# Turning softmax probabilities with a diagonal of reciprocal sums instead of the identity, in a two-block attention kernel

## The reference

```
s = einsum('bqhgd,bkhd->bhgqk', qg, k) * d ** -0.5      # + window mask, bias or sink column
p = softmax(s, axis=-1)
o = einsum('bhgqk,bkhd->bqhgd', p, v)
```

## Time and profile before

| | |
|---|---|
| median of 3 runs | 1799.63 us (1799.13 to 1804.88) |
| the profiled execution | 1798.95 us |
| its span | 1797.2 us |
| PE busy | 1690.1 us (94%) |
| DVE busy | 1037.0 us (58%) |
| ACT busy | 834.2 us (46%) |

### The profile page before, as it was taken

One profiled execution on the slowest core, in us unless ns is written; L12 is line 12 of the kernel. 1 busy time (PEld: TensorE's weight loads), 2 busy tenths in 40 slices (PEclk: granted clock), 3 DMA queues, 4 the chain that ended last, 5 costly groups with the idle time before them and its releaser, 6 DMA issues.

```text
span 1797.2 us, 30868 instructions
## 1 busy us (share of the span) xinstructions
PE 1690.1 (94%) x12106; PEld 1488.1 (83%) x12106; DVE 1037.0 (58%) x1965; ACT 834.2 (46%) x1546; POOL 81.7 (5%) x90
## 2 busy tenths in 40 slices
PE   4999989999999989997799999988999998989998
PEld 1985566888888869974699999868999998789998
DVE  3436644634343454358565656665867657568775
ACT  3327744513232333236444445674545546755443
POOL 2100001000000012110000001000000000000000
PEclk8999999999999999999999999999999999999999
DMA  8818763433333333347356663613666536046662
GB/s 246 218 48 260 233 176 97 114 95 103 95 94 95 105 108 104 110 135 226 83 147 179 180 187 106 182 36 102 182 187 188 148 112 195 12 141 179 182 190 85
DMA packets 406255, 254.48 MB, mean 142 GB/s; under 512 B 8448, under 2 KB 405024, under 8 KB 406112
## 3 DMA queue, kind: packets, MB, share of 16 engines
q1 hardware_dynamic: 404576, 248.80, 47.3%
q0 software_dynamic: 1536, 3.71, 0.8%
HBM read 251.36 MB, written 1.11 MB: 140 GB/s over the span
## 4 chain that ended last, share of the span: by engine, by line
PE 88%; DVE 6%; ACT 3%; issue 2%; DMA 2%; SPq 0%; DVEq 0%; ACTq 0%
PE bank L2143 72%; PE bank L2353 3%; PE bank L2364 3%; PE bank L2374 2%; PE bank L2266 2%; PE bank L2154 2%; PE bank L2122 2%; DVE parts L1118 1%; PE bank L2348 1%; DMA H<-ctx_t 1%; PE bank L2380 1%; PE bank L2389 1%; ACT parts L1301 1%; PE bank L2299 1%; DMA raw<-ada_w 0%
## 5 line engine op out<-in xcount | busy, mean ns | idle before, releaser
L2143 PE MATMUL bank<-AT,parts 128*128 128x256 f32 (+1 forms) x4704 | 680.1, 307 | 14.7 <-DVE AT L1104 7.6
L2143 PEld LDWEIGHTS bank<-AT,parts 128*128 128x128 f32 x4704 | 636.2, 192 | 56.9 <-issue 18.2
L1301 ACT ACTIVATE parts<-raw 128x1024 fp32r<-128x1024 f32 (+1 forms) x368 | 368.8, 1040 | 333.9 <-PE bank L2143 319.5
L1118 DVE TENSOR_TENSOR parts<-raw,parts 128x1024 fp32r<-128x1024 f32 (+1 forms) x368 | 434.9, 1213 | 147.0 <-ACT parts L1301 146.9
L2143 PE MATMUL bank<-HID,parts 128*128 128x256 f32 (+1 forms) x2592 | 400.2, 316 | 9.1 <-DVE HID L1800 9.1
L2143 PEld LDWEIGHTS bank<-HID,parts 128*128 128x128 f32 x2592 | 367.1, 192 | 40.3 <-DVE HID L1800 9.7
L2143 PE MATMUL bank<-parts,AT 128*128 128x256 f32 x2112 | 261.6, 285 | 12.3 <-DVE WORK L1935 6.7
L2143 PEld LDWEIGHTS bank<-parts,AT 128*128 128x128 f32 x2112 | 257.9, 193 | 14.7 <-DVE WORK L1935 7.2
L2023 DVE SCALAR_TENSOR_TENSOR H<-bank,MOD,H 128x256 f32<-128x256 f32 x120 | 52.5, 479 | 156.1 <-PE bank L2143 156.1
L1301 ACT ACTIVATE TOK<-bank 128x512 f32<-128x512 f32 (+2 forms) x160 | 71.3, 488 | 143.2 <-PE bank L2143 113.0
L2008 DVE TENSOR_TENSOR PR<-PR 128x512 f32<-128x512 f32 x48 | 33.1, 690 | 114.3 <-ACT PR L1545 114.3
(11 more groups left out here) (199 smaller groups left out, 1267.8 us busy)
## 6 DMA issues: line engine op xcount, KB each, us to landing
raw<-mlp_w SPq DMA_DIRECT2D x128, 512.0 KB, 4.2
raw<-ada_w SPq DMA_DIRECT2D x96, 512.0 KB, 4.8
raw<-w_up SPq DMA_DIRECT2D x88, 512.0 KB, 4.8
raw<-w_in SPq DMA_DIRECT2D x32, 512.0 KB, 4.5
raw<-w_down SPq DMA_DIRECT2D x32, 512.0 KB, 4.3
raw<-odd_w_in SPq DMA_DIRECT2D x24, 512.0 KB, 4.1
raw<-w_out SPq DMA_DIRECT2D x16, 512.0 KB, 4.8
raw<-even_w_in SPq DMA_DIRECT2D x12, 512.0 KB, 9.6
```

Source lines behind the costliest of these rows:

```text
L1118: ng.tensor_tensor(chunk_part(c, 1), chunk_raw(c), chunk_part(c, 0).bitcast(F32), ALU.subtract)\
L1301: return nc.scalar.activation(o, i, ACT.Copy)
L2143: ins = MM(out, stay, move, start=opens and kt == 0 and i == 0, stop=kt == kts - 1 and i == 2 and stops)
```

## The change

The reciprocals move ahead of the turn. For each step DVE takes the reciprocals of its two row sums, and scales the identity by each of them into a diagonal matrix in DIAG (four places of 128 x 128). PE then turns a tile by an ordinary float32 product, tile.T times diagonal, so that the turned probabilities come out normalised. The reciprocals' products in PE, ROOTS, OUT and the multiplication at the output fall away: ACT takes the high part straight from the values' bank, and DVE the low part, in a unit `four_low` that now stands at the head of the next odd iteration, ahead of `diag` and the score maxima. Kind D keeps its transposes.

```
+            if size == 2 and i % 2 and i > 4:
+                add("four_low", st=value)
+            if size == 2 and 0 <= i - 2 < n:
+                y = add("diag", four=steps[i - 2])
...
         if size == 2:
-            add("flush", ("flush", jobs[0]["layer"]), layer=jobs[0]["layer"])
+            add("four_low", st=value)
...
@@ ACT
-                elif k == "value" and x.four or k == "flush":
-                    if k == "value":
-                        filled(act, x.u)
-                        copy(ROOTS[:, x.c % 2, :], b[:, N:2 * N]).then_inc(root_turned, 1)
...
-                        copy(four_to(y, 0), OUT[:, y.c % 4, :]).then_inc(head_high, 1)
+                elif k == "value" and x.four:
+                    filled(act, x.u)
+                    copy(four_to(x, 0), b[:, 0:N]).then_inc(head_high, 1)
...
@@ DVE
-                        V.reciprocal(to, den).then_inc(root_ready, 1)
...
-                        V.tensor_tensor(OUT[:, x.c % 4, :], b[:, 0:N], ROOTS[:, x.c % 2, :], ALU.mult).then_inc(drained, 1)
...
+                elif k == "diag":
+                    for j in x.four:
+                        consumed(dve, index[("score", j["j"], 0)].u)
+                    if x.c >= 2:
+
+                        filled(dve, max(index[("turn_p", j["j"])].u for j in diags[x.c - 2].four))
...
+                    step(V.reciprocal(RD[:, i:i + 2], den))
+                    settle()
+                    for n in range(2):
+                        V.tensor_scalar(diag_of(x, n), ident, RD[:, i + n:i + n + 1], None, ALU.mult)\
+                            .then_inc(diag_ready, 1)
+                elif k == "four_low":
+                    y = x.st
+                    dve.wait_ge(head_high, y.c + 1)
+                    V.tensor_tensor(four_to(y, 1), bank[:, y.u % BANKS, 0:N], four_to(y, 0).bitcast(F32), ALU.subtract)\
+                        .then_inc(bank_drained[y.u % BANKS], 1)
...
@@ PE
-                            consumed(pe, s.u)
+                            n = j["diag"].four.index(j)
+                            pe.wait_ge(diag_ready, 2 * j["diag"].c + n + 1)
...
+                            if j["kind"] == "D":
+                                last = nc.tensor.transpose(b[:, o:o + P], p, ident)
+                            else:
+                                last = MM(b[:, o:o + P], p, diag_of(j["diag"], n), start=True, stop=True)
...
-                    pe.wait_ge(root_ready, x.c + 1)
-                    for v in range(TB):
-                        for i in range(2):
-                            r = roots(x)[1][:, 2 * v + i:2 * v + i + 1].broadcast_to([P, HD])
-                            last = MM(bank[HD * i:HD * i + HD, x.u % BANKS, N + v * P:N + v * P + P], r, ident, start=True,
-                                      stop=True, tile_position=(0, HD * i))
```

More of the change, by code:

```diff
@@ L234, in attention @@
                 add("mix", ("mix", j["j"]), job=j)
+            if size == 2 and i % 2 and i > 4:
+                add("four_low", st=value)
+            if size == 2 and 0 <= i - 2 < n:
+                y = add("diag", four=steps[i - 2])
+                for j in y.four:
+                    j["diag"] = y
             for j in steps[i] if i < n else ():
@@ L490, in plan @@
     for pos, x in enumerate(units):
-        if x.kind not in ("ada_row", "ahead", "post", "tail", "apply", "mix", "soft", "flush", "prep", "rstd", "final"):
+        if x.kind not in ("ada_row", "ahead", "post", "tail", "apply", "mix", "soft", "four_low", "diag", "prep", "rstd", "final"):
             x.u = u
@@ L536, in plan @@
             count["conv"] += 1
+        if x.kind == "diag":
+            x.c = count["diag"]
+            count["diag"] += 1
         if x.kind == "mix":
@@ L795, in two_block_kernel @@
         fours = [x for x in units if x.kind == "value" and x.four]
+        diags = [x for x in units if x.kind == "diag"]
         for x in fours:
@@ L987, in four_to, with fours_of @@
             return AT[:, part, ft, lo:lo + N]
-        def fours_done(layer, ft):
-            return max(x.c for x in fours if x.layer_of == layer and x.ft_of == ft) + 1
+        def fours_of(layer, ft):
+            return [x for x in fours if x.layer_of == layer and x.ft_of == ft]
         def turned_o_to(x):
@@ L1016, in resid_wait @@
                 else:
-                    pe.wait_ge(head_low, fours_done(layer, kt))
+                    for y in fours_of(layer, kt):
+                        consumed(pe, y.u)
             elif x.group[0] == "relu2":
@@ L1969, in _ @@
                     V.scalar_tensor_tensor(p1, p2, ratio, p1, ALU.mult, ALU.add).then_inc(comb_ready, 1)
-                elif k == "turn_p" and x.job["kind"] != "D":
-                    y = x.job["of"]
-                    if x.four[-1] is y.four[-1]:
-                        for j in y.four:
-                            consumed(dve, index[("score", j["j"], 0)].u)
-                        i, to = roots(y)
-                        den = DEN[:, i:i + 4]
-                        if y.job["kind"] in ("A", "CA"):
-                            step(V.tensor_tensor(ES[:, i:i + 4], ES[:, i:i + 4], den, ALU.add))
-                            settle()
-                            den = ES[:, i:i + 4]
-                        V.reciprocal(to, den).then_inc(root_ready, 1)
-                elif k == "value" and x.four or k == "flush":
-                    if k == "value":
-                        filled(dve, x.u)
-                        dve.wait_ge(root_turned, x.c + 1)
-                        V.tensor_tensor(OUT[:, x.c % 4, :], b[:, 0:N], ROOTS[:, x.c % 2, :], ALU.mult).then_inc(drained, 1)
-                        last = [x.c - 2] if x.c - 2 >= index[("value", first_four[x.job["layer"]])].c else []
-                    else:
-                        last = [last_four[x.layer].c - 1, last_four[x.layer].c]
-                    for c in last:
-                        y = fours[c]
-                        dve.wait_ge(head_high, c + 1)
-                        V.tensor_tensor(four_to(y, 1), OUT[:, c % 4, :], four_to(y, 0).bitcast(F32), ALU.subtract)\
-                            .then_inc(head_low, 1)
@@ new lines, in _ @@
+                elif k == "diag":
[3 more added lines that the diff above has]
+                        filled(dve, max(index[("turn_p", j["j"])].u for j in diags[x.c - 2].four))
+                    i = index[("score", x.four[0]["j"], 0)].nm % 8
+                    den = DEN[:, i:i + 2]
+                    if x.four[0]["kind"] in ("A", "CA"):
+                        step(V.tensor_tensor(ES[:, i:i + 2], ES[:, i:i + 2], den, ALU.add))
+                        settle()
+                        den = ES[:, i:i + 2]
+                    step(V.reciprocal(RD[:, i:i + 2], den))
+                    settle()
+                    for n in range(2):
[6 more added lines that the diff above has]
+                        .then_inc(bank_drained[y.u % BANKS], 1)
+                elif k == "value" and x.four:
+                    pass
@@ L2373, in _ @@
                         for i in range(2):
[L2374 to L2381 removed]
+                            last = MM(bank[HD * i:HD * i + HD, x.u % BANKS, 0:N], values_of(x.four[i])[t],
+                                      turned_pair(x, i, t), start=t == 0, stop=t == tiles - 1, tile_position=(0, HD * i))
                 elif k == "value":
```

22 lines of the change are left out of this document (7 added, 15 removed).

## The result

The changed kernel takes 1863.03 us (median of 4 runs, 1860.77 to 1865.19) against 1799.38 for the kernel before (4 runs, 1798.87 to 1804.88). The ratio is 1.0338, with a 95% interval of 1.0318 to 1.0358: slower by 63.6 us, where 48.5 were forecast. The profiled execution took 1864.81 us with a span of 1863.0, 65.8 more than the span before.

What follows compares the result with a forecast made beforehand. PE was taken as the limit before, a ring through DVE and ACT after. Layers 2 and 3 add 24 us and layer 0 24.5, so 48.5 on 1798.95 gives 1847.5, said as 1848; range 1825 to 1864.

Steps and rivals of the forecast that it cites:

- The ring: Attention loop once per four: ACT's values copy, DVE's low part, diagonals, PE's turn, ACT's copy, exponentials; sets the pace, not PE.
- The sign of being wrong that the prediction gave for DVE's row: Score maxima, now behind the diagonals, release the exponentials later than the copies do, making the ring longer than forecast.
- PE's own work: PE in three attention stages: 320 turned tiles add 35.2 us, dropped reciprocals' products save 14.4, so 20.8 us more.
- the forecast's own bounds: Whole kernel 1834 to 1860 us: diagonal 3 us, kind B 5, per-tile price 2, unseen slack 6.
- The ring of kind N, 5.5: Layers 2 and 3, kind N: 1.35 + 1.03 + 0.63 + 1.10 + 1.37 = 5.5 us per four, against 4.0 before.
- The start: Start of layer 3's attention: diagonals about 1.3 us late, first turns 1.8 more at half clock; 3 us.
- Layer 0's groups: Layer 0's attention: groups of kind A 17.4 us, of B some 15.7, against 13.65 before; 24.5 us with start and drain.
- Some slack may be found that my ring does not show: Attention stages: hidden slack might take back a fifth of what the ring adds beyond PE, 6 us.
- Only PE's work: Attention stages: low part never late, so only PE's added work counts; 1820 or 1822 us; chance 0.14.
- Faster: Turn on PE: product's second record hides behind weight loads, diagonals ready in time; saves 14.4 to 17.3 us, 1783; chance 0.05.
- The fourfold tile: Turn on PE: a turned tile costs four times the transpose, 112 us more, 1911; chance 0.02.
- The clock stays low: Layers 2 and 3: gaps at each four keep PE at granted clock 0.50, 31 us more, 1879; chance 0.04.

Runs made afterwards that it cites:

- the square: Kernels before and after plus four variants: turn by transposes or products, with output normalised, nothing normalised, or turn waiting for diagonals; ratios 0.9935 to 1.0338.
- the second look: The changed kernel run again unaltered for a second profile; 1861.95 us in one run, span 1860.2.
- kernel 4: The changed kernel without reciprocals, diagonals or their wait, turned by the product with the plain identity, nothing normalised; 1819.57 us, ratio 1.0104.

## Why the prediction was right and wrong

**The direction, the mechanism and PE's work were right.** The ring was named with its order of links, and in kind N the trace has those, but for the stretch between the two turns, where DVE's row and not PE's is the later path. The sign of being wrong that the prediction gave for DVE's row, maxima that release the exponentials later, did not come: ACT's exponentials wait 6.3 us in all for the maxima in the changed kernel, 15.8 in the kernel before. PE's own work was forecast at 20.8 us; the kernel with that alone came out at 0.0104 x 1800 = 18.7. By stretch it was 13.0, 2.3 and 2.4, where the terms of the prediction give 192 x 0.11 - 16 x 0.45 = 13.9 and twice 64 x 0.11 - 8 x 0.45 = 3.4. The parts were each a little large, and their errors cancel in part: the product costs 0.097 per tile by the square (0.11 forecast), the dropped products and their cover 12.5 us (14.4 forecast). Where PE sets the pace, in layer 0's steady groups, a tile does cost 0.110; the average is lower because in layers 2 and 3 part of the work falls into gaps that PE has anyway.

**The term that was too small is what the ring adds beyond PE's work.** The forecast of 48.5 holds 48.5 - 20.8 = 27.7 for it; the square gives 42. That the time still lies inside the range is in part luck: the forecast's own bounds ended at 1860 (the ones named add up to 10 us, so 1858), and only the step from there to 1864, for which no term was given, takes it in. By stretch, after less work alone, it is 15.0, 11.8 and 14.8 (19.7, 13.1 and 10.5 in the second look), where the prediction had 24.5 - 13.9 = 10.6 and twice 12 - 3.4 = 8.6. Three places make the difference, in the prediction's own steps:

- *The ring of kind N, 5.5.* It is 5.75. My turn until the next scores (1.03) took 1.06, but from the scores to the next turn it is 0.75, not 0.63, since that turn waits for its own diagonals at the end of DVE's row; and its end, copy, exponentials and copy add up to 1.16 + 1.39 = 2.55, not 2.47. From the first values to the last (1587.62 to 1627.04) layer 3 takes 39.4 us against 28.16, so 11.3 more, where 8.5 and 1 for kind M were forecast. The start was right in size: 11.84 us from the second pair of scores (1575.78) to the first values (1587.62), against 9.01, so 2.8 more where I gave 3 (11.04, 2.0 more, in the second look). The end was not: PE waits 1.43 and 0.99 ahead of its last turn and values, and in the first profile the values run at half pace (1.97 instead of 1.08).
- *Layer 0's groups.* Six periods from 148.76 to 251.41 take 102.65 us, 17.1 each, while the mean of my 17.4 and 15.7 is 16.5. (The same six take 83.16 before, 13.9 each and not 13.65, so the growth is 3.2 per group against a forecast mean of 2.9.) Kind A's first two periods are 18.1 and 17.7, not 17.4, its third 16.7. Kind B's are 16.5 to 16.9, not 15.7. PE's work alone takes 15.8 there in kernel 4 (15.4 by my terms), and the wait adds 0.7 to 1.1 where I gave it a few tenths: the fill units hide less of the ring than I thought. The stage's start and end, for which I gave 1.5, are 3.7 and 4.8 longer than before, with two groups' growth in them; the wait of 5.89 behind the splitting of weights is there (the longest at that place before was 3.00), and the prediction had no term for it. The prediction asked for diagonals behind the low part alone; the run with the low part later shows that DVE's whole row ahead of them (maxima, negatives, sinks, reciprocals) is late at the turn of a 512-key step.
- *"Some slack may be found that my ring does not show."* I lowered the range for it. The experiment with two low parts shows that there is hardly any: 14.5 us for 14.4 of added work. In the other direction there was more to find, since 24 us of the wait are left with the low part ahead of the diagonals out of the way; behind the maxima it closes a second ring.

**The rivals.** Only PE's work: no, though as a number it is close to the term that it names (18.7 for 20.8). Faster: no; not even with everything free of waits, since a product needs 0.097 us more per tile and pays back 12.5 us in all against 31. The fourfold tile: the product costs 0.097 more on a transpose of 0.107 to 0.117, so it takes 1.8 to 1.9 times as long (1.9 to 2.0 by the 0.110 of layer 0's steady groups). The rival's 1911 also left out the 14.4 us that go away. The rule in the Trainium skill, "TensorE: Matmul & The Clock Gate", section Terms, of a transpose mode 4 times faster for float32 does not hold for this shape here. The clock stays low: not through the stage (granted clock 1.00 from 1590 to 1622, in spite of a wait of 0.9 to 1.2 at each four), but twice at a stage's end in the first profile, behind the wait of 5.89 us in layer 0 (0.50) and behind the last waits of layer 3 (0.52 from 1627 to 1629); this is part of the missing microseconds, some 2 us at the first (3.75 against 2.02) and 1 at the second.

**"Every stage without attention should keep its length"** was nearly right. In the first profile they are 6.5 us longer, in the second 2.1. The two differ by the granted clock in stretches whose instructions are the same. What sets it from one execution to the next was not tried.

What stays open: whether some other order of DVE's row beats the kernel before. The square says that it can't with the product while the rest stands as it is (1.0104 with no wait at all). In-place scaling on DVE would have to win back over 17 of the 29 us that lie between it (1817.56) and the kernel that normalises nothing (1788.9). None of the seven experiments that normalise ahead of the turn beat the kernel before.

## What to carry to other kernels

When a change moves a small operation ahead of another engine's work, write down every link from that operation back to itself over the in-order queues, and give each the time from its row. Give links to both engines where two of them run side by side: here DVE's row was the later path between the two turns. The operation's own price (0.48 us per step for the diagonals) says little; waiting for it made 42 of the 64 us here. Taking away the late work ahead of it gave 16 to 18 of them back. Moving it does not help by itself, though: the work may start another wait, as the early diagonals did. And first ask what the ceiling is. The dropped work was worth 12.5 us with nothing put in its place, and the price of the product as the trace gave it ahead of time (0.1 us on 320 tiles) already exceeded it.

## What the runs showed of the hardware

- Work and waiting on the same engine added up in sum, within an interval of some 5 us (0.0166, 0.0169, 0.0171 for the product in three surroundings). In the steady groups of layer 0 they did not quite: 144 products cost 16.3 and 15.8 us with no wait for diagonals and 12.9 with it. The price of a product is not the same everywhere either: with no wait it was 18.9 us for 192 tiles in layer 0 (0.098 each), and 4.9 and 4.7 for 64 tiles in layers 2 and 3 (0.075), where PE has gaps without it.
- After a wait of 5.89 us the next turn ran at a granted clock of 0.50, while waits of 0.9 to 1.2 at each four left it at 1.00. At the ends of stages two executions of the same kernel differed: the last values of layer 3 ran at 0.52 in one and at 1.00 in the other, behind the same waits of 1.43 and 0.99.
- GpSimd took 0.72 us for a power of -1 on two columns, against 0.16 for DVE's reciprocal of the same two, and 0.62 for a 128 x 128 multiply by a column, where DVE takes 0.28. In place on 128 x 256 it was 0.93 against 0.35. (The profile's spans on GpSimd are rough.)
- In spite of its longer row on DVE (43.7 us of scaling in place against 30.9 for the diagonals), scaling in place on DVE with transposes was the cheapest of the ways tried to normalise ahead of the turn (1.0092).
